# Two rows of a transformer kernel (weight times gate) spread over the partitions by DMA through a scratch tensor, in place of transposes on TensorE

## The reference, cut to what matters

```python
mod = jax.nn.silu(c) @ w_ada[l] + b_ada[l]
shift_m, scale_m, gate_m, shift_f, scale_f, gate_f = jnp.split(mod, 6, axis=-1)
...                                     # norm, modulation, w_in, attention of two kinds
o = jnp.concatenate([o_n, o_m], axis=-1) @ w_o[l]
x = x + gate_m[:, None, :] * rms_norm_2(o, post_norm_mix[l])
h = modulate(rms_norm_2(x, pre_norm_ffn[l]), shift_f, scale_f)
f = jnp.square(jax.nn.relu(h @ w_up[l])) @ w_down[l]
x = x + gate_f[:, None, :] * rms_norm_2(f, post_norm_ffn[l])
```

## Time and profile before

| | us |
|---|---|
| median of 3 runs (2628.95 to 2631.02) | 2630.39 |
| the profiled execution, its own time | 2634.3 |
| its span in the profile | 2632.5 |
| TensorE busy | 2598.5 (99% of the span) |
| VectorE busy | 1749.8 (66%) |
| ScalarE busy | 1231.9 (47%) |
| GpSimd busy | 16.5 (1%) |

### The profile page before, as it was taken

How to read it: one execution, slowest core, us unless ns; L and a number is a source line. 1 busy time by engine, 2 the same in 40 slices (tenths; PEclk the granted TensorE clock), 3 DMA queues, 4 the chain that set the end, 5 groups by cost and what they waited for, 6 DMA issues and landing times.

```text
span 2632.5 us, 34546 instructions
## 1 busy us (share of the span) xinstructions
PE 2598.5 (99%) x12160; PEld 2164.5 (82%) x12160; DVE 1749.8 (66%) x2105; ACT 1231.9 (47%) x1476; POOL 16.5 (1%) x24
## 2 busy tenths in 40 slices
PE   9999999999999999999999999999999999999998
PEld 7888888888888888888888888888778887888886
DVE  6776768666556777777777777875665555555565
ACT  6444456454454444444444544555544443444443
POOL 0000000000000000000000000000000000000000
PEclk9999999999999999999999999999999999999999
DMA  8876667576667777787877577774467666766664
GB/s 296 273 239 210 206 206 232 181 228 223 193 191 249 254 253 254 255 255 255 253 252 253 179 239 231 219 221 147 139 213 218 212 212 193 230 211 213 208 215 137
DMA packets 281096, 582.40 MB, mean 221 GB/s; under 512 B 17904, under 2 KB 28288, under 8 KB 280336
## 3 DMA queue, kind: packets, MB, share of 16 engines
q1 hardware_dynamic: 279376, 574.38, 68.7%
q0 software_dynamic: 1600, 6.38, 0.8%
HBM read 578.57 MB, written 2.11 MB: 221 GB/s over the span
## 4 chain that ended last, share of the span: by engine, by line
PE 92%; DVE 3%; DMA 3%; ACT 1%; issue 1%; SPq 0%; DVEq 0%; POOL 0%; ACTq 0%
PE acc L1147 85%; PE W L1147 4%; DMA raw<-in_w_in 1%; PE W L1196 1%; DVE wlo L1616 1%; DMA raw<-in_w_ada_t 1%; ACT whi L556 1%; PE W L1318 0%; DVE arena L2230 0%; DMA arena<-in_xT 0%; DVE raw L1629 0%; DMA arena<-in_rel_rev 0%; PE acc L1460 0%; DVE rr L1855 0%; DVE arena L1792 0%
## 5 line engine op out<-in xcount | busy, mean ns | idle before, releaser
L1616 DVE TENSOR_TENSOR wlo<-raw,whi 128x1024 fp32r<-128x1024 f32 x888 | 1080.0, 1223 | 755.0 <-ACT whi L556 752.7
L556 ACT ACTIVATE whi<-raw 128x1024 fp32r<-128x1024 f32 x888 | 934.1, 1059 | 1123.6 <-PE acc L1147 960.4
L1147 PE MATMUL acc<-whi,hH 128*128 128x512 f32 x2528 | 689.3, 394 | 8.7 <-issue 4.5
L1147 PE MATMUL acc<-wlo,hH 128*128 128x512 f32 x2528 | 677.5, 390 | 2.3 <-DVE wlo L1616 2.3
L1147 PE MATMUL acc<-whi,hL 128*128 128x512 f32 x2528 | 676.8, 389 | 0.1
L1147 PEld LDWEIGHTS acc<-wlo,hH 128*128 128x128 f32 x2528 | 474.7, 188 | 103.1 <-DVE wlo L1616 3.6
L1147 PEld LDWEIGHTS acc<-whi,hL 128*128 128x128 f32 x2528 | 474.4, 188 | 101.1 <-DVE hL L1671 1.0
L1147 PEld LDWEIGHTS acc<-whi,hH 128*128 128x128 f32 x2528 | 468.8, 188 | 104.5 <-issue 11.9
L1147 PE MATMUL acc<-whi,yH 128*128 128x512 f32 x992 | 269.5, 393 | 0.0
L1147 PE MATMUL acc<-wlo,yH 128*128 128x512 f32 x992 | 265.4, 389 | 0.0
L1147 PE MATMUL acc<-whi,yL 128*128 128x512 f32 x992 | 265.4, 389 | 0.0
(11 more groups left out here) (192 smaller groups left out, 961.2 us busy)
## 6 DMA issues: line engine op xcount, KB each, us to landing
raw<-in_w_in SPq DMA_DIRECT2D x264, 512.0 KB, 4.7
raw<-in_w_ada_t SPq DMA_DIRECT2D x192, 512.0 KB, 4.9
raw<-in_w_ffn_in SPq DMA_DIRECT2D x176, 512.0 KB, 4.5
raw<-in_w_up SPq DMA_DIRECT2D x128, 512.0 KB, 4.5
raw<-in_w_down SPq DMA_DIRECT2D x128, 512.0 KB, 4.4
raw<-in_w_ffn_out SPq DMA_DIRECT2D x88, 512.0 KB, 4.9
raw<-in_w_out SPq DMA_DIRECT2D x32, 512.0 KB, 4.5
raw<-in_w_o SPq DMA_DIRECT2D x32, 512.0 KB, 3.7
```

The source lines that it names most:

```text
L556: act.activation(whi[:, v], raw[:, s], ACT.Copy).then_inc(S("w_hi"), 1)
L1147: return pe.matmul(o, l, r, start=start, stop=stop, skip_group_check=True)
L1616: dve.tensor_tensor(wlo[:, v], raw[:, s], whi[:, v].bitcast(F32), ALU.subtract)\
```

## The change

TensorE's `spread` and ACT's `row_copy` are taken out with their hooks. POOL gets a function `row(n, a)`, called for both rows. It waits for `row_cols`, writes `modA[:, a]` to the scratch tensor with the 2048 numbers in their order (64 B from each partition, in HBM single numbers of 4 B with 512 B between those of one partition), waits for that to land (`row_out`), waits until `rowB` is free (the last attention job, or the four products of the first row), and then reads the 8 KB row back into all 128 partitions of `rowB`, 1 MB. DVE's `by_row` waits for that DMA. The call for the first row stands between POOL's two memsets, and the one for the second row behind them.

```diff
             pool.memset(hid.rearrange("p k g c -> p (k g c)"), 0.0).then_inc(S("hid_zero"), 1)
+
+            def row(n, a):
+
+                pool.wait_ge(S("row_cols"), n + 1)
+                pool.dma_start(bass.AP(scratch.tensor, 0, [[1, P], [P, KT]]), modA[:, a],
+                               allow_slow_non_contiguous=True).then_inc(S("row_out"), 16)
+                pool.wait_ge(S("row_out"), 16 * (n + 1))
+                if n:
+                    pool.wait_ge(S("by_row"), 4)
+                else:
+                    pool.wait_ge(S("att_pv"), N_M)
+                pool.dma_start(rowB, bass.AP(scratch.tensor, 0, [[0, P], [1, D]])).then_inc(S("row_in"), 16)
+            pool.wait_ge(S("hk_in"), 16)
+            row(0, 1)
             pool.wait_ge(S("h_lo"), 12)
             pool.memset(blk(0, 2), 0.0).then_inc(S("o_zero"), 1)
+            pool.wait_ge(S("row_in"), 16)
+            row(1, 3)
...
-            group(4, hooks={3: row_copy(0)})
-            group(4, hooks={1: square_o(0), 3: row_copy(1)})
+            group(4)
+            group(4, hooks={1: square_o(0)})
...
-            for ahead, then in ((6, row_copy(2)), (4, row_copy(3))):
-                for _ in range(ahead):
-                    hi()
-                then()
+            for _ in range(10):
+                hi()
...
-                hooks = {2: lambda: spread(i, 1)} if i < 2 else {}
-                group(4, hH, hL, frees[i:i + 1], ready=pair_ready(8), hooks=hooks)
+                group(4, hH, hL, frees[i:i + 1], ready=pair_ready(8))
...
-            down2(8, (("f2_sum", 27), ("f2_sum", 28)), {0: {2: lambda: spread(2, 3)}, 1: {2: lambda: spread(3, 3)}}, last=True)
+            down2(8, (("f2_sum", 27), ("f2_sum", 28)), last=True)
...
-                    dve.wait_ge(S("row_in"), rows + (1 if c < 2 else 2))
+                    dve.wait_ge(S("row_in"), 16 * rows)
```

More of the change, by code:

```diff
@@ L1197, in turn @@
                 ins.then_inc(S(sem), 1)
[L1199 to L1208, removed]
             def busy(n):
@@ L2211, in _ @@
             for i in range(2, 4):
-                group(4, hooks={2: by_row(i - 2, ("o_sum", 0), 0), 3: wo_add(i - 1)})
+                group(4, hooks={2: by_row(i - 2, ("o_sum", 0), 1), 3: wo_add(i - 1)})
             pl.phase("ffn2_first")
@@ L2216, in _ @@
             then(scaled(2, "pre_ffn", 64, 1.0))
-            by_row(2, ("o_sum", 0), 0)()
+            by_row(2, ("o_sum", 0), 1)()
             lo(2)
             wo_add(3)()
-            by_row(3, ("o_sum", 0), 0)()
+            by_row(3, ("o_sum", 0), 1)()
             def post_norm(k, rows, sem, units=0):
```

## The result

The changed kernel is slower. Its median is 2637.48 us over 11 runs (2635.81 to 2640.39), that of the kernel before on the same chip 2631.16 (2628.95 to 2633.52, 11 runs). The ratio is 1.0024, with a 95% interval of 1.0016 to 1.0032: 6.3 us more, where 3.6 less were forecast. The profiled execution took 2638.98 us, its span is 2637.2; before 2634.3 and 2632.5, so the two profiles are 4.7 apart, somewhat less than the medians.

What follows compares the result with a forecast made beforehand. TensorE was taken to bound the kernel; four spreads at 0.905 us save 3.62, while removed ACT copies, added waits and DMA load count 0: 2630.39 - 3.62 = 2626.8 us, 0.14% less, range 2624.7 to 2629.8.

Steps and rivals of the forecast that it cites:

- The price of the removed spreads: Four spreads of transposes on TensorE, 0.905 us each including slower restart: 3.62 us saved.
- both halves reach the end: In front of the norms at output projection and last down projection: TensorE's saving counts whole, 1.81 us at each.
- The reads: Two 1 MB reads into rowB near 1839 and 2573: landing in 11.0 us, both rows in time, TensorE loses 0.
- (b): Second write lands slowly, so the second row is late: 2628.4 us at 27 us landing, 2636.4 at 35; 4 in 100.
- (c): The 1 MB reads make TensorE wait as near 415: 1.2 us more, 2628.0 us; 11 in 100.
- (d): Output projection's saving is swallowed because the norm behind starts by something else: 1.8 us lost, 2628.6 us; 6 in 100.
- the load of the writes on the DMA engines: Both small POOL writes beside the weights: 1.9 us of each engine, far inside 11.3 us, so costing 0.
- Rival (a): 4-byte writes at 1492.6 and 2566 hold DMA engines, weights late: TensorE loses X - 11.3 us at each; 8 in 100.
- bounded from above by 11.0: Second row's write: 4.9 us to landing chosen, 11.0 as upper end, the longest landing of the nearest trace rows.
- the cover: Lateness of weight loads that TensorE tolerates at the writes and reads: 4.2 plus 7.1, together 11.3 us.
- the part of 7.1 us behind ACT: ACT's rounding of weight units may be 7.1 us late before TensorE stands.
- the 4.2 us in front of ACT: Weight load for a raw slot lands with 4.2 us to spare before ACT wants it.

Runs made afterwards that it cites:

- experiment 1: Changed kernel with the first 4-byte write issued as soon as its row is there, ahead of POOL's memset: 2628.32 us, ratio 0.9985 to the kernel before.
- 2: Changed kernel with both writes in 128 pieces of 64 bytes, so the row's numbers come back in another order: 2627.72 us, ratio 0.9983 to the kernel before.
- 4: Changed kernel with each row turned by one TensorE transpose, copied by ACT and written in 16 pieces of 512 bytes: 2628.75 us, ratio 0.9986 to the kernel before.
- 7: Changed kernel with 64-byte pieces and the right order, by_row reading rowB with a step of 16 numbers: 2628.61 us, ratio 0.9991 to the kernel before.
- 9: Changed kernel with only 8 of 16 columns written, 1024 4-byte pieces 64 bytes apart in a larger tensor: 2626.91 us, ratio 0.9985 to the kernel before.
- experiment 8: Changed kernel with only 8 of 16 columns written, 1024 packed 4-byte pieces: 2633.92 us, ratio 1.0012 to the kernel before.
- 10: Changed kernel with 2048 4-byte pieces 8 bytes apart, neighbours from the same partition, in a larger tensor: 2643.63 us, ratio 1.0049 to the kernel before.
- experiment 6: Changed kernel with both 4-byte writes issued by SP in its hardware queue among the weight loads, reads still from POOL: 2640.17 us, ratio 1.0039 to the kernel before.

## Why the prediction was wrong

**The price of the removed spreads was right.** 3.62 us were forecast. Where no write made TensorE stand, the kernel is 3.5 us (experiment 1), 4.1 (2), 3.1 (4), 2.8 (7, with its slower products) and 5.0 (9) below the median of before on the same chip, each with some 2.4 to 3 us either way. That both halves reach the end was right too: 1.78 us came back at the output projection (from 8.05 to 6.27 behind), and 1.8 in the last down projection (from 6.45 to 4.63).

**The reads were right.** The first was issued at 1847.18, landed after 8.1 us, and TensorE was busy for 50.00 of 50.00 us from 1840 to 1890. The second was issued at 2587.58 and landed after 9.9, some 10 us before its `by_row` at 2607.54. Rivals (b), (c) and (d) did not happen.

**The step that failed is the load of the writes on the DMA engines**, taken as 0 from 1.9 us of engine time and 4.9 us to landing, the price of 2048 pieces of 96 bytes that are read the earlier trace rows. A write of 2048 pieces of 4 bytes lands after 12.7 to 16.4 us, and for about 9 us at the first and 11 at the second the engines move under 80 GB/s. The row was near in the number of pieces and far in what decides: small writes packed closely in HBM. The yardstick failed with it: the forecast took engine time as the load, and of that the write took 0.62 us, less than the 1.9 that was forecast, while the packets of the weights took twice their time. Rival (a) has the same yardstick in it ("X us of each engine"), and is met only if X is read as the landing time. The landing time was bounded from above by 11.0, of transfers with long pieces, which bounds nothing for this one. (A small slip beside it: landing is counted from the start of the issue, so the sum has the two issues of 1.20 us twice.)

**The second error is in the cover.** 11.3 us were worked out in a stretch without `w_ada_t`, and used for both writes. At the second it held, with little to spare: ACT waited 8.15 us and began 6.5 late (2592.85, where 2586.4 would have been its turn), and TensorE didn't stand. At the first, ACT would have begun at about 1498.9 and began at 1508.57, 9.65 late; TensorE stood for 2.70, so the part of 7.1 us behind ACT was right (9.65 - 2.70 = 6.95). But the 4.2 us in front of ACT were not there: the unit landed 9.4 us later than usual (14.0 against 4.6) and ACT was as much late. In the kernel before ACT waits for weights from 1505.9 on there. The cover was 7, not 11.3.

**Then the loss was multiplied.** Rival (a) was the right mechanism, with the slower side, place and cause, and had 8 in 100. It priced a late unit at its lateness, X - 11.3 at each write. Measured: nothing at the second, and 9.1 us at the first, of which the first stand is 2.70. The rest comes behind the stand: half clock, DVE with two remainders and two `w_ada_t` pieces to work off before its rotation, loads that still let ACT wait up to 3.5 us until 1530 (up to 2.9 in the kernel before), and a second stand 30 us later. In experiments 1 and 2, where no slow write stands at this place, all of it is gone.

The Trainium skill had spoken against the write ("DMA: Bandwidth & Descriptors", "Rules for kernel authors": a strided last dimension becomes one descriptor for each element). The runs agree that such a write is slow: with one piece for each partition it lands in 2.4 us, with sixteen in 14.6. The same page's "Specifications" say that transfers under 512 bytes are read, modified and written. That can't be the price by itself, since the pieces of 64 bytes are under 512 too. The 25.6 us that I estimated from its "Latency and other measured facts" with nothing overlapped are too high: 12.7 to 16.4 were measured. The forecast weighed that rule only as a late row, priced at 0.2 us, and not as a load on the weights' path.

What stays open: how the time for packed pieces comes about (experiments 8 and 10 show no simple law), why the weights' packets get slower beside them, and whether the second stand would have come without the first fall of the clock. By their starts 3.2 of the 9.1 us are low clock and 5.8 are stands and waits, but no run has the one without the other.

## What to carry to other kernels

Price a DMA by its pieces and its side (read or write, packed or apart), not by its bytes and not by its share of the engines' time: 8 KB with 0.6 us on each engine delayed the loads of another queue by 9 us. Where the trace has no transfer of that form, its price has no upper end there, and the slower side deserves a real chance; measure it alone, or choose a form that the trace shows. And work out the cover at the place of each transfer: the same write cost 9 us in a stage with thin DMA slack and nothing 29 us sooner, in front of a norm. And before moving a DMA to the list that issues the weights, look at what it waits for: every load behind it waits too (11.6 us in experiment 6).

## What the runs showed of the hardware

- Landing of small writes to HBM, median of the two in each run: 128 pieces of 64 bytes 2.4 us; 16 of 512 bytes 4.8; 1024 of 4 bytes, 64 bytes apart 4.0; 2048 of them 8.9; 1024 of 4 bytes packed 11.6; 2048 packed 14.6 (13.8 in each of two other runs); 2048 at a step of 8 bytes 17.1 (21.2 and 13.0). From 4.0 to 8.9 are 4.9 us for 1024 more pieces, 64 on each of 16 engines: an estimate of 77 ns for one, if they are spread evenly.
- The write's own packets took 3.1% of 20 us of the engines with the pieces packed and with them 64 bytes apart. Packed, SP's queue moved 2.39 MB in 69.4% of the engines' time; in the kernel before it was 4.46 MB in 69.2%.
- Issue on POOL grows with the number of pieces: 0.55 us for 128, 0.91 for 1024, 1.18 for 2048.
- The granted clock fell to half behind stands of TensorE of 2.70 and 2.37 us in the changed kernel; behind one of 2.72 in experiment 8 it stayed at 1.00.
- A DVE product with an operand stepped by 64 bytes took 1955 ns in place of 1220 for 128x1024.
